# The sample's pass goes ahead of the prompt's: a reordered two-layer kernel with a fifth expert tile at its end

## What is computed

```python
for l in range(DEPTH):
    mod_ctx = _adaln(c_ctx, w_ada[l], b_ada[l])
    xp, ckv_p, kr_p = _layer(xp, mod_ctx, lp, None, None)          # prompt, alone
    mod_lat = _adaln(c, w_ada[l], b_ada[l])
    xs, _, _ = _layer(xs, mod_lat, lp, rope, (cache_ckv[:, l], cache_krope[:, l]))
y_prompt, y_sample = _rmsnorm(xp, final_norm), _rmsnorm(xs, final_norm)

def _layer(...):                       # dense part, then experts
    h = _rmsnorm(x) * (1 + scale1) + shift1
    # w_in -> latent attention (8 heads) and a Hyena long convolution with filters
    # computed by a small network; both projected, gated, merged, w_out
    x = x + gate1 * (merged @ w_out)
    h2 = _rmsnorm(x) * (1 + scale2) + shift2
    # for each token 8 heads x 16 experts: q = h2 @ peer_wq, scores against 2 x 128 keys,
    # top 16 of each, top 16 of their sums, softmax g; then
    # out = sum over the 128 experts of gelu(h2 . u_e) * g_e * v_e
    x = x + gate2 * _peer(h2)
```

## Time and profile before

| | |
|---|---|
| median of the runs | 4986.13 us (4980.84 to 4996.76) |
| span of the profiled execution | 4993.9 us; by its own time it lies 8 us over the median |
| busy, share of the span | PE 79%, PE weight loads 40%, DVE 69%, ACT 17%, POOL 34% |
| granted TensorE clock, mean | 0.911 of full speed |
| DMA | 1585.7 MB, mean 318 GB/s; 1355 MB of it on the queue of the gathers |
| chain that ended last | DMA 18%, PE 17%, DVE 13% of the span |

### The profile page before, as it was taken

One profiled execution on the slowest core, in us unless ns is written; L12 is line 12 of the kernel. 1 busy time (PEld: TensorE's weight loads), 2 busy tenths in 40 slices (PEclk: granted clock), 3 DMA queues, 4 the chain that ended last, 5 costly groups with the idle time before them and its releaser, 6 DMA issues.

```text
span 4993.9 us, 40260 instructions
## 1 busy us (share of the span) xinstructions
PE 3933.8 (79%) x12034; PEld 2006.4 (40%) x12034; DVE 3458.2 (69%) x9168; ACT 871.4 (17%) x2434; POOL 1674.7 (34%) x1437
## 2 busy tenths in 40 slices
PE   7887789797988866767777579799797777777776
PEld 3437464345433333324533246445442232222222
DVE  0333788857877867777677878877787767766665
ACT  1221241001111112211111123110111111111111
POOL 0230132332233434544434223234134444433432
PEclk9879889899999988988988789999998899999999
DMA  7325376765699989999999667767479999999998
GB/s 266 116 80 205 131 270 262 276 252 212 248 363 418 402 362 401 415 410 399 406 410 421 273 228 254 295 233 280 168 276 385 380 419 380 399 397 421 422 422 346
DMA packets 223333, 1585.71 MB, mean 318 GB/s; under 512 B 26678, under 2 KB 29026, under 8 KB 32012
## 3 DMA queue, kind: packets, MB, share of 16 engines
q0 software_dynamic: 186784, 1354.97, 67.8%
q1 hardware_dynamic: 36332, 228.18, 11.9%
HBM read 1571.74 MB, written 11.30 MB: 317 GB/s over the span
## 4 chain that ended last, share of the span: by engine, by line
DMA 18%; PE 17%; DVE 13%; issue 4%; ACT 2%; POOL 1%; DVEq 0%; POOLq 0%; ACTq 0%
DMA sb_arena<-in_peer_uv,sb_idx 12%; PE ps L1105 9%; DMA sb_gbufs<-in_peer_uv,sb_idx 5%; PE ps L1004 4%; DVE sb_gbufs L1861 2%; DVE sb_arena L1861 2%; DVE sb_eacc L1884 1%; PE ps L719 1%; PE ps L1042 1%; DMA sb_ring<-in_w_oab 1%; DVE sb_arena L1845 1%; POOL sb_gbufs L2104 1%; DVE sb_arena L1847 1%; PE ps L862 1%; ACT sb_dge L1368 1%
## 5 line engine op out<-in xcount | busy, mean ns | idle before, releaser
L2104 POOL DMA_INDIRECT sb_gbufs<-in_peer_uv,sb_idx x768 | 946.2, 1232 | 1934.3 <-PE ps L1105 886.3
L1105 PE MATMUL ps<-sb_gbufs,sb_dge 128*128 128x512 f32 x1856 | 931.1, 653 | 358.3 <-ACT sb_dge L1368 358.0
L1105 PE MATMUL ps<-sb_arena,sb_dge 128*128 128x512 f32 x1856 | 911.6, 641 | 278.3 <-ACT sb_dge L1368 274.3
L2104 POOL DMA_INDIRECT sb_arena<-in_peer_uv,sb_idx x512 | 571.7, 1117 | 834.2 <-PE ps L1105 793.4
L1861 DVE CUSTOM_DVE_ANT_0 sb_gbufs<-sb_gbufs,sb_keep 128x1024 f32<-128x1024 f32 x512 | 621.3, 1227 | 302.3 <-DMA sb_gbufs<-in_peer_uv,sb_idx 300.2
L1861 DVE CUSTOM_DVE_ANT_0 sb_arena<-sb_arena,sb_keep 128x1024 f32<-128x1024 f32 x512 | 620.2, 1224 | 290.8 <-DMA sb_arena<-in_peer_uv,sb_idx 289.3
L1105 PEld LDWEIGHTS ps<-sb_gbufs,sb_dge 128*128 128x128 f32 x1856 | 370.9, 208 | 884.0 <-issue 442.5
L1105 PEld LDWEIGHTS ps<-sb_arena,sb_dge 128*128 128x128 f32 x1856 | 362.9, 204 | 789.7 <-ACT sb_dge L1368 394.8
L1363 ACT ACTIVATE sb_small<-sb_small 128x2 f32<-128x2 f32 x512 | 104.6, 204 | 2211.4 <-DVE sb_small L1872 2186.4
L1884 DVE SCALAR_TENSOR_TENSOR sb_eacc<-sb_gbufs,sb_small,sb_eacc 128x1024 f32<-128x1024 f32 x299 | 388.2, 1298 | 9.4 <-DVE sb_small L1895 0.5
L1368 ACT ACTIVATE sb_dge<-sb_ident,sb_small 128x128 f32<-128x128 f32 x928 | 328.2, 396 | 123.6 <-DVE sb_small L1958 120.1
(11 more groups left out here) (257 smaller groups left out, 4315.5 us busy)
## 6 DMA issues: line engine op xcount, KB each, us to landing
sb_ring<-in_w_ada SPq DMA_DIRECT2D x48, 1024.0 KB, 4.8
sb_ring<-in_w_wq SPq DMA_DIRECT2D x32, 1024.0 KB, 8.4
sb_ring<-in_w_hy SPq DMA_DIRECT2D x24, 1024.0 KB, 4.9
sb_ring<-in_w_ga SPq DMA_DIRECT2D x16, 1024.0 KB, 5.0
sb_ring<-in_w_gb SPq DMA_DIRECT2D x16, 1024.0 KB, 12.9
sb_ring<-in_w_oab SPq DMA_DIRECT2D x16, 1024.0 KB, 5.1
sb_ring<-in_w_out SPq DMA_DIRECT2D x14, 1024.0 KB, 9.0
sb_gbufs<-in_peer_uv,sb_idx POOLq DMA_INDIRECT x768
```

The costliest lines, as they stand in the source:

```text
L1105: q = pe.matmul(ps[:, c, :], dge[:, b, :], gbuf[b][:, D + c * 512:D + c * 512 + 512], start=(h == 0 and i == 0), stop=(h == HALVES - 1 and ...
L2104: nc.gpsimd.indirect_dma_start(out=gbuf[b], out_offset=None, in_=I["peer_uv"], in_offset=bass.IndirectOffsetOnAxis(ap=idx[:, col:col + 1], ...
```

## The change

The order of the two groups is turned round. `DENSE` is now sample, prompt, sample, prompt. There are two phases, one for a layer. Layer 0: modulation steps (A) with an F behind each; five F; then the sample's dense steps with the remaining F between the first of them, and no experts beside; then the sample's experts with modulation 1 and the prompt's dense pass 0 between them. Layer 1: the sample's dense pass with the prompt's experts of layer 0; then the sample's experts with the prompt's dense pass 1 between them; then the prompt's experts of layer 1 as a fifth tile of the same steps (V), on PE's path and not on DVE's. `by_vector` now holds for tiles 2 to 4 of both layers. The routing pieces of layer 1 follow the same spacing as those of layer 0. Modulation vectors are kept for each layer; the final norm's row and sums move to other places of SBUF. Cut to its core:

```diff
+LAST = 1
 STEPS_S = (TILES - 1) * HALVES
+STEPS = [STEPS_S, STEPS_S + HALVES]
-DENSE = [(layer, g) for layer in range(DEPTH) for g in GR]
+DENSE = [(layer, g) for layer in range(DEPTH) for g in GR[::-1]]
@@ weight_loads
-        if not g.latent:
-            out += [((d, "ada", i), 2048, None, ("ada_ps", layer * 24 + i + 1)) for i in range(24)]
+    out = modulation(0)
...
+        if not g.latent and layer + 1 < DEPTH:
+            out += modulation(layer + 1)
@@ by_vector, tile_at
-    return 1 if layer < DEPTH - 1 and m >= HALVES and m % TOKEN == TOKEN - 1 else 0
+    return 1 if HALVES <= m < STEPS_S and m % TOKEN == TOKEN - 1 else 0
+def tile_at(p):
+    return p if p < TILES else 0
@@ phases
-    first = ["P"] * (ADA_POINTS + 2) + ["P", "F"] * FILTER_POINTS
-    out = [("p", 0, first + ["P"] * (ADA_POINTS + len(GR[0].pace()) - first.count("P")))]
...
-        order = spread(pace, 0 if layer else 5, UNITS * (PAIRS + 1), end - 0.005)
-        if layer == 0:
-            for k, n in ((4, 1), (3, 1), (2, 1), (1, 2)):
-                order[k:k] = ["R0"] * n
+        if layer:
+            order = spread(pace, 0, UNITS * (PAIRS + 1), end - 0.005)
+        else:
+            order = ["A", "F"] * ADA_POINTS + ["F"] * 5 + ["D"] + ["F"] * 3 + ["D", "F", "F"] * 4
+            order += ["F"] * (FILTER_POINTS - order.count("F"))
+            order += ["D"] * (len(pace) - order.count("D"))
...
-        points, given, last = (len(GR[0].pace()) if more else 0), 0, TOKENS_S - 10
+        points, given, last = len(GR[0].pace()), 0, TOKENS_S - 10
-        for m in range(8, TOKENS_S + 1):
+        for m in range(8, STEPS[layer] // TOKEN + 1):
             order.append("V")
-            if between and (m % 3 != 2 if more else (m < 12 or m % TOKENS >= 10) and m % 3 == 0):
+            if between and m % 3 != 2:
                 order.append(between.pop(0))
             if m < TOKENS + 3 and early:
-                order.append("P")
+                order.append("A")
                 early -= 1
-            if m > TOKENS + 3 and points:
+            if m > TOKENS + 3 and given < points:
...
-            if more and TOKENS_S - 7 <= m < TOKENS_S - 2:
+            if TOKENS_S - 7 <= m < TOKENS_S - 2:
                 order.append("R0")
@@ follow
+                parts = {"D": dense(2 * layer), "P": dense(2 * layer + 1), "V": expert_step("s", layer), "G": first_gathers(layer)}
+                if layer == 0:
+                    parts["F"], parts["A"] = spectra(), chain(adaln(0), adaln(1))
                 else:
+                    parts["E"] = expert_step("p", layer - 1)
@@ DVE, expert_step: the fifth tile takes the prompt's h2 and gate
-                for m in range(STEPS_S):
-                    t, h = 1 + m // HALVES, m % HALVES
+                for m in range(STEPS[layer]):
+                    p, h = 1 + m // HALVES, m % HALVES
+                    t = tile_at(p)
...
-                        dot("s", layer, m * HALF + i, q + i, h2s[:, t - 1, :])
+                        dot("s", layer, m * HALF + i, q + i, h2s[:, t - 1, :] if t else h2p[:, :])
@@ POOL, expert_step
-                        if n + NB < (TILES - 1) * SLOTS:
+                        if n + NB < STEPS[layer] * HALF:
                             gather("s", layer, n + NB)
```

More of the change, by code:

```diff
@@ L153, in weight_loads, with modulation @@
 def weight_loads():
-    out = []
+    def modulation(layer):
+        return [((2 * layer, "ada", i), 2048, None, ("ada_ps", layer * 24 + i + 1)) for i in range(24)]
+    out = modulation(0)
     for d, (layer, g) in enumerate(DENSE):
         nt = g.nt
-        if not g.latent:
-            out += [((d, "ada", i), 2048, None, ("ada_ps", layer * 24 + i + 1)) for i in range(24)]
+        if not g.latent and layer + 1 < DEPTH:
+            out += modulation(layer + 1)
         at = START[d]
@@ L230, in expert_slots @@
     for layer in range(DEPTH):
[L231 to L234, removed]
-        for m in range(STEPS_S):
+        if layer:
+            for n in range(SLOTS):
+                take(("p", layer - 1, n), n % 4)
+                dve_n += 1
+                out["p", layer - 1, n] = (n % 4, used[n % 4], "acc", dve_n)
+        for m in range(STEPS[layer]):
             own = HALF - by_vector(layer, m)
@@ L523, in meet, with follow @@
             eng.wait_ge(Z["arrived"], 4 * k)
[L525 to L527 removed]
+        def follow(eng, dense, expert_step, route, first_gathers, spectra, adaln, ahead=False):
+            for k, (layer, order) in enumerate(PHASES):
                 if k:
                     meet(eng, k)
[L530 to L542 removed]
+                parts = {"D": dense(2 * layer), "P": dense(2 * layer + 1), "V": expert_step("s", layer), "G": first_gathers(layer)}
+                if layer == 0:
+                    parts["F"], parts["A"] = spectra(), chain(adaln(0), adaln(1))
+                else:
+                    parts["E"] = expert_step("p", layer - 1)
+                for tile in range(TILES):
+                    parts[f"R{tile}"] = route(tile, layer)
                 for name in dense_first(order) if ahead else order:
@@ L1095, in expert_step @@
                         pe.wait_ge(*busy.pop(b))
-                for m in range(STEPS_S):
-                    t, h = 1 + m // HALVES, m % HALVES
-                    if h == 0 and t > 1:
-                        pe.wait_ge(Z["acc_read"], layer * (TILES - 1) + t - 1)
+                for m in range(STEPS[layer]):
+                    p, h = 1 + m // HALVES, m % HALVES
+                    if h == 0 and p > 1:
+                        pe.wait_ge(Z["acc_read"], layer * (TILES - 1) + p - 1)
                     own = HALF - by_vector(layer, m)
@@ L1117, in first_gathers @@
                 yield
-            follow(pe, dense, expert_step, route, first_gathers, spectra, ahead=True)
+            follow(pe, dense, expert_step, route, first_gathers, spectra, adaln, ahead=True)
         @block.scalar
@@ L1138, in dense @@
                 s, v, at, nt, T = S, views[g.name], counted(d), g.nt, g.T
-                if not g.latent:
-                    yield from adaln(layer)
+                mod, fold = mods[layer], folds[layer]
                 if not g.latent and layer:
@@ L1350, in expert_step, with squares @@
                     return
[L1351 to L1360, removed]
+                def squares(p):
+                    t = tile_at(p)
+                    act.wait_ge(Z["x_done"], p)
+                    junk = h2s[:, t - 1, :] if t else h2p[:, :]
+                    act.activation(junk, x[:, t, :], ACT.Square, accum_out=st[:, 16 + t:17 + t]).then_inc(Z["fsq"], 1)
+                for m in range(STEPS[layer]):
+                    p, h = 1 + m // HALVES, m % HALVES
                     q = (m % GROUPS) * HALF
@@ L1397, in first_gathers @@
                 yield
-            follow(act, dense, expert_step, route, first_gathers, spectra)
+            follow(act, dense, expert_step, route, first_gathers, spectra, adaln)
         @block.vector
@@ L1481, in dense @@
                 s, v, at, nt, T = S, views[g.name], counted(d), g.nt, g.T
-                if not g.latent:
-                    for _ in range(ADA_POINTS - 1):
-                        yield
-                    mod_vectors(layer)
-                    yield
+                mod, fold = mods[layer], folds[layer]
                 dve.wait_ge(*at("ss1", nt))
@@ L1987, in dense @@
                 s, v, at, nt, T = S, views[g.name], counted(d), g.nt, g.T
-                if not g.latent:
-                    for _ in range(ADA_POINTS):
-                        yield
                 for _ in range(1 + nt + 1 + nt + 2 + nt * NH + 1):
@@ L2043, in dense, with adaln @@
                     yield
+            def adaln(layer):
+                for _ in range(ADA_POINTS):
+                    yield
             def filter_loads(f):
```

149 lines of the change are left out of this document (82 added, 67 removed).

## The result

The changed kernel takes 5114.38 us, median of four runs (5109.1 to 5115.58), beside 4985.26 us for the kernel before on the same chip: 1.0254 times as long, 95% interval 1.024 to 1.0269. Slower by 2.5%, where 3.3% was forecast. The profiled execution spans 5113.8 us.

What follows compares the result with a forecast made beforehand. Dense passes were taken as bound by PE, expert stages by DMA bytes. The terms 920 + 1632 + 682 + 1591 + 324 + 11 = 5160 us of span, less 8, gave 5152 us, 3.3% slower; range 5060 to 5225.

Steps and rivals of the forecast that it cites:

- (a): Opening to the sample's first turn of h2: modulation 115, filters 160, dense pass 645, together 920 us against 1207.
- (b): Sample's experts of layer 0 beside modulation 1 and the prompt's dense pass 0: 187 + 333 + 1112 = 1632 us.
- (c): Sample's dense pass 1 beside the prompt's experts of layer 0: 682 us, as today's stage.
- (d): Sample's experts of layer 1 beside the prompt's dense pass 1: 188 + 281 + 10 + 1112 = 1591 us, against 1462.
- (e): Fifth tile, the prompt's last experts beside nothing: 324 us, with ends 314 and 342.
- (f): Closing norm after the last tile's sum: stays at 11 us.
- The dense pass without experts: Sample's pass in the opening: 682 less some 37 is 645 us, ends 576 (PE's floor) and 682.
- The filters: Filter steps in the opening: 105 us of PE work plus 55 of waits, 160 us, ends 104 and 196.
- rival 1: Opening: filters and modulation hold each other up; filters 230, dense pass 670, tile 1 slower; 5267 us; chance 0.10.
- Rival 2: Sample's pass gains more from empty DVE: pass 600, filters 130, prompt pass at its bytes (+89); 5047 us; chance 0.15.
- Rival 3: Opening where PE never waits: 740 in place of 920; faster than before, 4932 us; chance 0.05.
- Rival 4: Layer 1: prompt's pass not hidden, tile 5's gathers wait behind late routing or h2; 32 to 60 us more, 5205; chance 0.10.

Runs made afterwards that it cites:

- a_eighth_weights: Changed kernel with only the first eighth fetched of 30 weight loads of the prompt's dense pass 1, 27.5 MB less: 5056.58 us, ratio 1.0129 to the kernel before.

## Why the prediction was right, point by point

The direction, the reason and the range held; the central time was 38 us high (5152 against 5114). In span it was 46 high (5160 against 5114), since the 8 us taken off for the profiled execution were not there in the changed kernel. The opening alone was 67 us high, and 23 us too little on the tiles of layer 1 hid a third of that: the total is nearer than its largest term by luck. By its own terms, in us of span, a tile's end being the addition to x:

| term | forecast | measured |
|---|---|---|
| (a) opening to the first turn of h2 | 920 | 853 |
| (b) experts 0 beside modulation 1 and prompt pass 0 | 1632 | 1632 |
| (c) sample's pass 1 beside the prompt's experts | 682 | 682 |
| (d) tile 1, with the query products | 479 | 494 |
| (d) tiles 2 to 4 beside prompt pass 1 | 1112 | 1120 |
| (e) fifth tile | 324 | 323 |
| (f) closing | 11 | 10 |

(b), (c) and (e) were taken whole from a row of the same work, and came out to a us or so. What was mis-sized is (a), in two terms.

The dense pass without experts was put at 645; with the experts left out of the kernel before it is 606. The waits that the prediction names, L894 and half of L767, come to 26 us and not to the 37 that it took off. It kept as the dense chain's own the softmax's 11.2 us (L821) and all of the second norm's 17.6 (L1030); with DVE empty these fall to 0.9 and 8.2, so they were DVE's queue too. And PE's 576 us of busy time is no floor: with the experts gone it is 558, at a clock of 0.97 for 0.93.

The filters were put at 160; 853 less 115 and 606 is 132. Here the clock is not the reason. PE's busy time in the filters' two products, L705 and then L1088, is 102 us, where 105 was taken:

```profile
0.00:303.00 303.00, 63.65 (x128) 24.75 (x128) 0.90 0.41 150
...
0.00:303.00 303.00, 38.23 (x64) 12.73 (x64) 0.90 0.41 150
```

What was too high is the idle time. 55 us were added for it, and 30 are left, 14.9 of them the wait for x (put at 12). The prediction kept the modulation at 115 us with its own idle inside and laid the filters' work behind that. But the filters' products also fill the modulation's waits: PE waits 9.1 us for w_ada (L691) in the changed kernel, 19.7 in the kernel before. That is 11 of the 25 us; the others are shorter waits of the filters themselves, by subtraction. Of the 67 us, then, some 21 are PE's busy time and 46 are waits.

Tile 1 of (d) was put at +10 for the routing pieces and measured +26: DVE is busy 260 of 305 us, as forecast, and DMA's share falls to 0.91 (0.94 before). That the routing pieces cost it is argued; no run took them out. The prompt's pass beside tiles 2 to 4 was +127 for +119; that it is mostly bytes is borne out by a_eighth_weights, an estimated 81 of 127. That the prompt's experts under a dense pass cost no time of their own except what they delay was too kind: they cost 75 us, 18 of them in PE's busy time.

The rivals: filters and modulation do not stand in each other's way (rival 1); separating them costs 51 us. Rival 2 had the opening right: it put the sample's pass at 600 and the filters at 130, measured 606 and 132. It failed in its other half, the prompt's pass at its bytes, 89 for 127, and so came out at 5047, 67 us low. Rival 3 needed an opening of 754 us; PE alone is busy 761 of the 853, so it was out of reach. Rival 4 did not happen: tile 4 takes 371 us, as tile 4 of layer 0 does (370), and tile 5 behind it 323 for 324.

The rule that put HBM to SBUF at some 358 GB/s for a core (the Trainium skill, "DMA: Bandwidth & Descriptors", Where 436 GB/s comes from) would have made the fifth tile an estimated 375 us; it took 323 at 406 GB/s, so the trace goes against the rule again. The rule that judges TensorE's headroom by MFU and LDWEIGHTS busy (the Trainium skill, "Perfetto Trace Analysis", Identifying the Most-Contended Engine) came out in between: the share of weight loads is 312 of 567, 55%, where PE is busy 93%, so nothing near the other half was to be had. But matmul busy was not the floor either: in the dense pass it shrank by 18 us with the same instructions.

## What to carry to other kernels

Where stages alternate between one bound by an engine and one bound by bytes, ask of each reorder what lies under what afterwards: the same 128 gathers cost 75 us under the compute-bound pass and 323 behind the byte-bound stage, and these 248 us outweigh the 127 that a serial pass gives when it leaves the front for the byte-bound stage. Take the stages that stay from rows of the same work, and price the two that change by leaving work out. Before fillers are moved, count the waits that they fill where they are, and a step moved forward needs its inputs moved forward with it: here the two edits together gave 0.5%, alone 0.0 and 0.1%. And when work is laid into a stage, count that stage's own waits as filled first: here 11 us of the modulation's.

## What the runs showed that was not expected

One wait can cost more than its length. PE's 15 us for x, taken away in the kernel before with its filters ahead, gave 23 us of span: the granted clock in the modulation went from 0.94 to 1.00 and behind it from 0.84 to 0.87, and PE's busy time fell by 4 and 6 us with the same work. In the changed kernel the same edit gave 15 us of span and no more, so the surplus is not a rule.

Half rows are not half the time for the DMA engines. With 8 KB a row the tile moves 406 GB/s at a busy share of 0.98; with 4 KB it moves 288 at 0.83. That is 0.24 against 0.29 of busy share for each 100 GB/s, 20% more for a byte. Since PE bounds the tile of half rows, no run shows what rate they would reach by themselves.
